# Layer hand-overs of a two-layer diffusion trunk: context sums, context order, window bands and lambda's exponential moved

## What is computed

```python
def ffn_half_step(xs, md, k, g, w_in, w_out):
    h = modulate(xs, g, md[3 * k], md[3 * k + 1])
    return xs + 0.5 * md[3 * k + 2] * swiglu(h, w_in, w_out)

def pool_mix(h, w, b, scale):      # four groups of 256 channels, windows 2, 4, 8, 16
    lo = jnp.clip(t - win // 2, 0, n)
    hi = jnp.clip(t - win // 2 + win, 0, n)
    mean = (cs[:, hi, grp] - cs[:, lo, grp]) / (hi - lo)
    d = mean - hf
    y = jnp.einsum('bngi,gio->bngo', d, w) + b
    return y * scale

lam = jnp.exp(jnp.sum(lp[0] * lp[1])) - jnp.exp(jnp.sum(lp[2] * lp[3])) + lam_init
```

## Time and profile before

| | |
|---|---|
| median of 3 runs | 2661.54 us (2659.71 to 2662.74) |
| the profiled execution | 2663.32 us, its span 2661.5 us |
| mean granted clock | 0.972 |
| PE busy | 96% of the span, 14907 matmuls |
| DVE, ACT, POOL busy | 53%, 31%, 17% |
| chain that ended last | PE 89%, DVE 5%, ACT 2%, POOL 1%, issue 2% |
| DMA | 30.6% of 16 engines, 89 GB/s |

### The profile page before, as it was taken

One profiled execution on the slowest core, in us unless ns is written; L12 is line 12 of the kernel. 1 busy time (PEld: TensorE's weight loads), 2 busy tenths in 40 slices (PEclk: granted clock), 3 DMA queues, 4 the chain that ended last, 5 costly groups with the idle time before them and its releaser, 6 DMA issues.

```text
span 2661.5 us, 39473 instructions
## 1 busy us (share of the span) xinstructions
PE 2550.5 (96%) x14907; PEld 2220.7 (83%) x14907; DVE 1418.7 (53%) x2114; ACT 835.3 (31%) x1207; POOL 444.1 (17%) x527
## 2 busy tenths in 40 slices
PE   6999999998899999999899999999799998899999
PEld 6788888887788888888788888888789986788887
DVE  6788666224688867872522222222677775433332
ACT  1333223212533323331322212211455553342221
POOL 2012111002211111110100000001377761000000
PEclk6899999999899999999999999999899999899999
DMA  6355443221055544442112212222101102233332
GB/s 217 107 151 159 137 128 101 63 76 43 17 158 152 159 119 143 140 132 63 36 59 63 73 53 63 62 72 57 48 25 47 47 16 57 70 95 97 92 104 86
DMA packets 363023, 238.58 MB, mean 90 GB/s; under 512 B 6769, under 2 KB 361682, under 8 KB 362962
## 3 DMA queue, kind: packets, MB, share of 16 engines
q1 hardware_dynamic: 361120, 237.00, 30.6%
q10 hardware_dynamic: 1842, 0.77, 0.1%
HBM read 235.65 MB, written 2.10 MB: 89 GB/s over the span
## 4 chain that ended last, share of the span: by engine, by line
PE 89%; DVE 5%; issue 2%; ACT 2%; POOL 1%; DMA 0%; SPq 0%; ACTq 0%; DVEq 0%; POOLq 0%
PE pu L1018 73%; PE pv L1230 5%; PE pu L1026 5%; PE pu L1267 1%; DVE h_lo L1601 1%; PE pv L1258 1%; PE pu L1248 1%; DVE xn L1593 1%; PE pv L1095 1%; DVE w_lo L1472 1%; POOL sqa L534 1%; DVE mx L1680 1%; PE pu L1354 1%; DVE a L1699 0%; ACT e L890 0%
## 5 line engine op out<-in xcount | busy, mean ns | idle before, releaser
L1018 PE MATMUL pu<-h_hi,w_hi 128*128 128x512 f32 x2384 | 668.5, 349 | 14.5 <-DVE w_lo L1472 14.5
L1018 PE MATMUL pu<-h_lo,w_hi 128*128 128x512 f32 x2384 | 663.6, 347 | 0.0
L1018 PE MATMUL pu<-h_hi,w_lo 128*128 128x512 f32 x2384 | 662.5, 346 | 0.0
L1472 DVE TENSOR_TENSOR w_lo<-w_raw,w_hi 128x1024 fp32r<-128x1024 f32 (+1 forms) x250 | 358.5, 1434 | 396.0 <-ACT w_hi L671 387.6
L671 ACT ACTIVATE w_hi<-w_raw 128x1024 fp32r<-128x1024 f32 (+1 forms) x250 | 284.4, 1140 | 705.7 <-PE pu L1018 673.5
L1018 PEld LDWEIGHTS pu<-h_hi,w_hi 128*128 128x128 f32 x2384 | 378.3, 189 | 75.5 <-DVE w_lo L1472 8.2
L1018 PEld LDWEIGHTS pu<-h_lo,w_hi 128*128 128x128 f32 x2384 | 379.0, 189 | 60.4
L1018 PEld LDWEIGHTS pu<-h_hi,w_lo 128*128 128x128 f32 x2384 | 378.1, 189 | 60.7
L1489 DVE SCALAR_TENSOR_TENSOR ada_acc<-ada_raw,cs,ada_acc 128x384 f32<-128x384 f32 x588 | 337.3, 615 | 10.7 <-DVE ada_acc L1489 1.8
L1018 PE MATMUL pu<-a_hi,w_hi 128*128 128x512 f32 x1100 | 305.7, 346 | 0.6
L1018 PE MATMUL pu<-a_hi,w_lo 128*128 128x512 f32 x1100 | 304.8, 345 | 0.0
(11 more groups left out here) (200 smaller groups left out, 2984.8 us busy)
## 6 DMA issues: line engine op xcount, KB each, us to landing
w_raw<-in_ffn_w_in SPq DMA_DIRECT2D x176, 512.0 KB, 3.9
ada_raw<-in_ada_w SPq DMA_DIRECT2D x84, 768.0 KB, 4.7
w_raw<-in_ffn_w_out SPq DMA_DIRECT2D x64, 704.0 KB, 4.6
w_raw<-in_diff_w_qkv SPq DMA_DIRECT2D x24, 512.0 KB, 5.3
first_h<-in_ada_w SPq DMA_DIRECT2D x4, 1536.0 KB, 19.7
w_raw<-in_diff_w_o SPq DMA_DIRECT2D x8, 512.0 KB, 3.9
first_own<-in_ada_w SPq DMA_DIRECT2D x2, 1536.0 KB, 19.0
xstage<-in_x SPq DMA_DIRECT2D x4, 512.0 KB, 5.3
```

Of the source, the lines that this page charges most:

```text
L1018: last = pe.matmul(banks(ch, s_), w[:, j, :], r[:, SEG[s_]], start=(j == 0 and i == 0), stop=(j == k - 1 and i == 2))
L1472: dve.tensor_tensor(w_lo[:, ch, 0:k * P], w_raw[:, ch, 0:k * P], w_hi[:, ch, 0:k * P].bitcast(F32), ALU.subtract).then_inc(split_ready[ch], 1)
```

## The change

Four moves, with no change of the arithmetic but its order:

1. In first_unit the context's sums stand behind channel 0's chunks 0 to 3 instead of both channels'; in project_first behind chunk 1 instead of 3. norm_rms of the other segment stands behind chunk 5 of norm_seg instead of 3 (in the tails of norms 3, 4 and 5 and in norm 2; not in norm 1).
2. In first_unit the context is made channel by channel, and each channel signals when it is done. In the first input pair of each FFN ACT makes w_hi of channel 0 ahead of silu; that pair stands outside the loop.
3. The exponential of lambda and nlam go behind head 0 of the attention.
4. POOL builds the windows behind the granules of FFN0, in tiles of their own; DVE makes the bands from them (make_bands) behind its modulation vectors, unscaled (window minus w times the identity), and 1/w goes into pscl. scale_windows and finish_bands go.

```diff
-        band_hold = sb("band_hold", [P, 6, NT], F32, pool)
+        band_ends = sb("band_ends", [P, 2, len(WINDOWS), P + HALO], F32, bands)
+        edge_cols = sb("edge_cols", [P, 2, len(WINDOWS), PAD], F32, bands)
+        win = sb("win", [P, 1 + len(WINDOWS), HELD], F32, wins)
@@ POOL
-                    if i == 1 and s_ == 0:
-                        build_windows()
-                    if i == 1 and s_ == 1:
-                        finish_bands()
             sum_chunks(0)
             granule_rests(0)
+            build_windows()
             sum_chunks(1)
@@ ACT
-            def silu_pair(pair, f, n, nxt, k, p, ada):
+            def silu_pair(pair, f, n, nxt, k, p, ada, hi_first=False):
                 act.wait_ge(unit_done[0], pair + 2)
+                if hi_first:
+                    split_hi(0, pair + 1, nxt)
                 for s in range(2 if n == NT else 1):
                     i = act.activation(sil[:, SEG[s]], ps(0, s), ACT.Silu)
                 i.then_inc(psum_used[0], 1)
-                split_hi(0, pair + 1, nxt)
+                if not hi_first:
+                    split_hi(0, pair + 1, nxt)
...
-                if i == 1:
-                    scale_windows()
...
+                    if q == 0:
+                        silu_pair(b, 0, n, DC, k, p0, [beside(k, p0, lag) for lag in (1, SUM_LAG)], True)
-                    for lo, hi, ada in spans(k, p0, 0, FP - 1, (1, SUM_LAG)):
+                    for lo, hi, ada in spans(k, p0, int(q == 0), FP - 1, (1, SUM_LAG)):
...
             norm_act(3)
+            ffn_act(2, None)
+
+            norm_act(4)
+            attn_act(0, True, False, False)
             act.wait_ge(lam_step, 2)
             act.activation(lam_s[:, 2:4], lam_s[:, 0:2], ACT.Exp).then_inc(lam_step, 1)
-            ffn_act(2, None)
-
-            norm_act(4)
-            attn_act(0, True, False, False)
             attn_act(1, True, True, False)
@@ PE, first_unit
                     for j in range(4):
                         pe.wait_ge(h_ready[0], DC * i + j + 1)
                         chunk_seg(i, ch, 0, j, DC, h_hi, h_lo)
-                if late_ctx:
-                    sums_most(i, 1)
-                    sums_last(i, 1)
+                    if late_ctx and ch == 0:
+                        sums_most(i, 1)
+                        sums_last(i, 1)
...
-                for j in range(DC):
-                    pe.wait_ge(h_ready[1], DC * i + j + 1)
-                    for ch in range(2):
+                for ch in range(2):
+                    for j in range(DC):
+                        pe.wait_ge(h_ready[1], DC * i + j + 1)
                         last = chunk_seg(i, ch, 1, j, DC, h_hi, h_lo)
-                        if j == DC - 1:
-                            last.then_inc(unit_done[ch], 1)
+                    last.then_inc(unit_done[ch], 1)
@@ PE, project_first
-                    if j == DC // 2 - 1:
+                    if j == 1:
                         sums_most(4, 1)
                         sums_last(4, 1)
@@ PE, mix_out and pool_pe
+                        band = (band_ends[:, 0, g] if t == t0 else band_ends[:, 1, g] if t == t1 - 1 else
+                                win[:, g + 1, HALO:HALO + BAND])
...
-                pe.wait_ge(band_ready, 3)
+                pe.wait_ge(band_ready, len(WINDOWS))
@@ DVE, tail_dve and pool_dve (norm 2)
-                                3: lambda: norm_rms(i, 1)})
+                                5: lambda: norm_rms(i, 1)})
@@ DVE
+            def make_bands():
+
+                dve.wait_ge(win_ready, 2 + len(WINDOWS))
+                dve.wait_ge(act_ready, FC + 1)
+                for e_, at in ((0, 2 * HALO), (1, 2 * HALO + P - PAD)):
+                    last = dve.tensor_tensor(edge_cols[:, e_], win[:, 1:, at:at + PAD], edge_sb[:, :, e_, :], ALU.mult)
+                mod_link(last)
+                for g, w in enumerate(WINDOWS):
+                    for e_, c0, p0 in ((0, 2 * HALO, 0), (1, HALO, P)):
+                        c1 = c0 + P + HALO
+                        dve.scalar_tensor_tensor(band_ends[:, e_, g], win[:, 0, c0:c1], -float(w), win[:, g + 1, c0:c1],
+                                                 ALU.mult, ALU.add).then_inc(mod_step, 1)
+                        mod_steps[0] += 1
+                        dve.wait_ge(mod_step, mod_steps[0])
+                        cols = win[:, 0, c0 + p0:c0 + p0 + PAD]
+                        dve.scalar_tensor_tensor(band_ends[:, e_, g, p0:p0 + PAD], cols, -float(w), edge_cols[:, e_, g],
+                                                 ALU.mult, ALU.add)
+                    dve.scalar_tensor_tensor(win[:, g + 1, HALO:HALO + BAND], win[:, 0, HALO:HALO + BAND], -float(w),
+                                             win[:, g + 1, HALO:HALO + BAND], ALU.mult, ALU.add).then_inc(band_ready, 1)
...
+            for g, w in enumerate(WINDOWS):
+                for s_ in range(2):
+                    last = dve.tensor_scalar(pscl[:, s_, 2 * g:2 * g + 2], pscl[:, s_, 2 * g:2 * g + 2], 1.0 / w, None, ALU.mult)
+            mod_link(last)
             dve.wait_ge(in_par2, 16 * N_PAR2)
+            make_bands()
...
             ffn_dve(2, None)
+            tail_dve(4, lambda b: head_w_lo(0, b))
+            norm_seg(4, 1, {})
+            attn_dve(0, True, False, False)
             dve.wait_ge(lam_step, 3)
             dve.tensor_tensor(nlam[:], lam_s[:, 3:4], lam_s[:, 2:3], ALU.subtract).then_inc(lam_step, 1)
...
-            tail_dve(4, lambda b: head_w_lo(0, b))
-            norm_seg(4, 1, {})
-            attn_dve(0, True, False, False)
```

More of the change, by code:

```diff
@@ L186, in build @@
         a_hold = sb("a_hold", [P, 2 * FP * NT], F32, over)
+        bands = ExitStack()
+        band_ends = sb("band_ends", [P, 2, len(WINDOWS), P + HALO], F32, bands)
+        edge_cols = sb("edge_cols", [P, 2, len(WINDOWS), PAD], F32, bands)
+        bands.close()
         sil = sb("sil", [P, NT])
@@ L573, in build_windows @@
                     gp.wait_ge(win_ready, g + 2)
-                    nc.gpsimd.tensor_tensor(shifted(g + 1, c0, c1), shifted(g, c0 + up, c1 + up),
-                                            shifted(g, c0 - down, c1 - down), ALU.add).then_inc(win_ready, 1)
-            def finish_bands():
-                gp.wait_ge(in_par2, 16 * N_PAR2)
-                gp.wait_ge(win_scaled, len(WINDOWS))
-                for e_, at in ((0, HALO), (2, HALO + P - PAD)):
-                    cols = band_sb[:, :, e_, at:at + PAD]
-                    nc.gpsimd.tensor_tensor(cols, cols, edge_sb[:, :, e_ // 2, :], ALU.mult).then_inc(band_ready, 1)
-                gp.wait_ge(band_ready, 2)
-                one = shifted(0, HALO, HALO + BAND).unsqueeze(1).unsqueeze(1).broadcast_to((P, len(WINDOWS), 3, BAND))
-                nc.gpsimd.tensor_tensor(band_sb[:], band_sb[:], one, ALU.subtract).then_inc(band_ready, 1)
+                    nc.gpsimd.tensor_tensor(win[:, g + 1, c0:c1], win[:, g, c0 + up:c1 + up],
+                                            win[:, g, c0 - down:c1 - down], ALU.add).then_inc(win_ready, 1)
             def inv_rms_tokens(i, s_):
@@ L803, in norm_hi @@
                                bias=mod[:, mod_seg(i, s_), sh:sh + 1]).then_inc(hhi_ready[s_], 1)
-            def scale_windows():
-                for g, w in enumerate(WINDOWS):
-                    act.wait_ge(win_ready, g + 3)
-                    act.activation(band_sb[:, g], shifted(g + 1, HALO, HALO + BAND).unsqueeze(1).broadcast_to((P, 3, BAND)),
-                                   ACT.Copy, scale=1.0 / w).then_inc(win_scaled, 1)
             def pool_act():
@@ L985, in _ @@
             norm_act(3)
-            act.wait_ge(lam_step, 2)
-            act.activation(lam_s[:, 2:4], lam_s[:, 0:2], ACT.Exp).then_inc(lam_step, 1)
             ffn_act(2, None)
@@ L991, in _ @@
             attn_act(0, True, False, False)
+            act.wait_ge(lam_step, 2)
+            act.activation(lam_s[:, 2:4], lam_s[:, 0:2], ACT.Exp).then_inc(lam_step, 1)
             attn_act(1, True, True, False)
@@ L1629, in pool_dve @@
                 norm_seg(POOL_NORM, 0, {0: lambda: split_lo(0, PAIR_POOL + 1, DC), 1: pool_end,
-                                        2: lambda: split_lo(1, PAIR_POOL + 1, DC), 3: lambda: norm_rms(POOL_NORM, 1)})
+                                        2: lambda: split_lo(1, PAIR_POOL + 1, DC), 5: lambda: norm_rms(POOL_NORM, 1)})
                 norm_seg(POOL_NORM, 1, {})
```

16 lines of the change are left out of this document (7 added, 9 removed).

## The result

The median is **2641.6 us** (4 runs, 2640.2 to 2643.9) against 2661.8 us in the same comparison: ratio 0.9925, 95% interval 0.9914 to 0.9937, 20 us faster. I had said 2638.5 us with a range of 2630 to 2652. The profiled execution took 2642.95 us, its span 2641.1 us at a mean clock of 0.973 (0.972 before).

The account below looks back on a forecast made before the run. PE, busy 96% of the span, bounds the kernel, so gains lie only where it waits or runs at the lower clock. Terms: -3.7 + 1.2 - 11.3 - 8.1 - 1.2 = -23.1 us, forecast 2638.5 us, range 2630 to 2652.

Parts of the forecast that it names:

- the forecast case: Whole kernel: a gain of 17 to 31 us, chance 0.56.
- rival 1: Context stretch, FFN1 to FFN3: the clock falls in channel 0, giving 7.5 to 12 us back, 2646 to 2651; chance 0.26.
- Term A: Pool start: without POOL's band step DVE's slow w_lo goes and PE starts sooner, -3.7 us (0 to -4.7).
- Term B: Ahead of the pool's tail add: 30 band instructions on DVE delay PE's first sums, +1.2 us (0 to +3).
- Rival 3: DVE ahead of the tail add: bands hold up the tail, slower, 2667 us or more; chance 0.03.
- Term C: FFN1 to FFN3 and the projection: context sums moved up spare PE's wait, -11.3 us (-5 to -18).
- Rival 2: First units: the sums' wait only moves to chunks 6 and 7, the gain shrinks to 3 or 4, 2646; chance 0.10.
- Term D: First units of FFN0 to FFN3: context by channel shortens the way to the second unit, -8.1 us (-12 to 0).
- FFN2's share of D: FFN2's context by channel: gains 2.3 us, two table loads included, and 1.6 more from the clock behind it.
- Term E: Attention: lambda's exponential at head 0's end moves its table load into idle time, -1.2 us (0 to -1.3).

Follow-up runs that it names:

- the second profile: The changed kernel profiled again with nothing altered; that repeat measured 0.993 (0.9917 to 0.9944) of the kernel before.
- fillers: Changed kernel plus two unread 256-column products per chunk, chunks 0 to 6, in channel 0's context of FFN1 to FFN3's first units: 0.9905 of the kernel before.

## Why the prediction was right, and where not

The time was 3.1 us over the forecast and inside the range; the forecast case held, with rival 1 in it at a fraction of its price. Some luck is in the number: 0.9 us of the profiled gain came in stretches where nothing was changed, mostly as loops with fewer long chunks.

- **Term A** (3.7): 3.6 in the changed kernel and with the bands alone. The slow w_lo went with POOL's work, and no other wait took its place.
- **Term B** (1.2): 1.0. The slack ahead of the tail add was as counted. Rival 3 fell: the 30 operations took 0.17 us each on average, not 1.1.
- **Term C** (11.3): 10.6 (9.6 by the second profile). DVE's wait for the sums fell by 18.4 us, and the spreads come 10.6 us sooner. Rival 2 did not come: from the sums to the spread PE waited for nothing, and DVE then stood 6.41 us at the spread. FFN2 was the smallest, 1.6, as it was with the sums alone (1.7).
- **Term D** (8.1): 4.5, **the step that failed.** "So FFN1 gains 0.7" counted PE's 24 products of channel 1 at 0.12 us, 2.9 in all. 13 of them ran at 0.21, the 24 took 4.2 us, and FFN1 lost 1.0, FFN3 0.9 where 0.4 of gain stood. The step took the clock from the rows of the kernel before, where six products per chunk filled the stretch; with three the idle time between them let it fall (x12 in 3.4 us, then 0.50). With fillers FFN1 gains 0.5 of the 0.7.
- **Rival 1's price** (7.5 to 12) was too high by a factor of two to nearly four: 3.3 us inside the three stretches. I had let channel 1 run wholly at 0.50 and the next unit for a while too. But the clock came back while channel 1 was made: in FFN1 behind 13 of its 24 products, in FFN3 behind 14, in FFN2 behind two. It was at 1.00 by 729.9, before the second unit at 731.2. PE went on into that unit without a wait, so what the clock cost was paid in full and not hidden behind w_hi, silu and w_lo (in FFN3 all but the 0.26 us that PE waits there with the fillers). The 1.6 us of clock behind the second unit of FFN2 and FFN3 did arrive.
- FFN2's share of D had the right size and an owner too many: the table load's absence alone gives 1.6 and 1.5. Booked to lambda, step 3 is worth some 4 us (5.1 measured alone), and the order by channel too little for medians to show (put back, 0.9931 with 0.9914 to 0.9948, against 0.9925 and 0.993). In the single profiles, with the long chunks' share taken off, the four FFNs, from their spread to the next tail or the end, take together 4.6 us more with the order put back, 3.2 of it in FFN0, where the clock then fell as well. Behind such a piece of idle time it does not fall every time, so this figure is one draw.
- **Term E** (1.2): 1.8, and 1.0 alone. Among all profiles this stretch runs from 368.2 to 373.1 us, so the size is not firm.
- **The table load** took 1.28 us, and the next activation began 0.01 to 0.02 us behind it, in FFN2, the attention and FFN3. The 2.66 us with drain that the Trainium skill states ("ScalarE: Activation LUTs", What ACT_TABLE_LOAD costs), and that would have cost FFN3 1.4 us more, are not seen here.

## What to carry to other kernels

When a reorder makes PE wait piece by piece for its inputs, price the work behind the wait at the lower clock as well. Here idle time spread over many short products cost 0.5 to 2.1 us a place, and a piece of 2 to 4 us ahead of a full unit some 1.5 us behind it, each when the clock fell. Whether it fell could differ at the same place with the same idle time, so one profile of a kernel shows that the clock can be lost there, not how often. And cut the trace into stretches between the same instructions to judge a part of some 2 us: most of the short ones repeat to 0.1 us where the clock is the same, while medians of whole runs moved by 5 us and more between kernels that differ by less. In the long loops, count the two paces before you compare.
